# A decoder layer on one core: the mixer's x1 goes straight to the output tensor, and the last stage adds the expert sums to it with accumulating stores

## The chip, the core and the metric

The kernel runs on one core of a Trainium2 chip. The core has five engines that run side by side and wait for each other by semaphores: PE (TensorE, matrix multiply), DVE (VectorE, elementwise), ACT (ScalarE, activation functions), POOL (GpSimd) and SP (SyncE, which here only issues transfers). Sixteen DMA engines, shared by all who issue transfers, move data between the core's own memory (SBUF, 128 partitions) and the chip's main memory (DRAM). The metric is the time of one execution on the device, in microseconds (us).

## What is computed

One layer of a decoder, 2048 tokens of 1024 f32 values each:

```python
h = rms_norm(x, g_pre_mix) * (1.0 + sc1) + sh1
proj = h @ w_in
y = concat([conv_module(...), hgrn2(...)]) @ w_out
x = x + gt1 * rms_norm(y, g_post_mix)            # this x is "x1" below

h = rms_norm(x, g_pre_ffn) * (1.0 + sc2) + sh2
y = hier_moe(h, ...)                             # per token 2 of 32 experts, weighted sum
x = x + gt2 * rms_norm(y, g_post_ffn)            # the output
```

`rms_norm(y, g)` is `y * rsqrt(mean(y*y) + 1e-6) * g`, one mean per token. The last line is what the changed stage computes: `x1 + grow2 * y / rms(y)`, with `grow2 = gt2 * g_post_ffn`, a row of 1024 values.

## The kernel before

The work is cut into 16 tiles of 128 tokens; a tile of 128 x 1024 f32 is 0.524 MB (512 KB), 4 KB in each partition. Four phases follow one another, each in a block of its own that all engines leave together.

**Mixer** (`mixer_phase`, to about 1210 us). Four blocks of 512 tokens. Here x1 is made on DVE in the tile `yt`, and POOL stores it to DRAM (L321, 16 stores), stores the normalised `xn` (L323) and clears the tensor `y` in DRAM with zeros (L325). `ap["x1"]` names the DRAM tensor that takes x1: an internal tensor `x1_dram`.

**Routing** (`routing_phase`, to about 1265 us) chooses two experts for each token and lists blocks of 128 rows by expert.

**Experts** (`expert_phase`, about 1265 to 1789 us). 48 blocks run. For each, POOL fetches 128 rows of `xn` with an indirect transfer (L1547). PE turns them and multiplies by the expert's gate and up weights (L1614 to L1616), then by the down weights (L1626). The product, weighted on ACT, is added to `y` in DRAM by an indirect transfer that accumulates, issued by POOL (L1563). That is an `indirect_dma_start` with `compute_op=ALU.add`. Each of these waits for the one before it. The weights of an expert are 3 MB (gate 1 MB, up 1 MB, down 1 MB), loaded by SP into three slots (L1428, L1429, L1434) once an earlier expert has left its slot. In SP's program, after every three experts, comes one `load_x1` (L1504). It brings two tiles of x1, 1 MB, from DRAM into `x1_all`, an SBUF array that holds all 16 tiles. There are 8 of these loads.

**Combine** (`combine_phase`, from about 1789 us). SP loads `y` tile by tile into a ring of 8 places `ys` (L1850). Per tile, ACT squares and sums it (L1829), takes a logarithm (L1831) and an exponential (L1833), which gives the reciprocal of the root of the mean. DVE multiplies the tile by that and by `grow2` (L1842), then adds it to the x1 tile in SBUF (L1845). SP stores the result to `out` (L1856) and then issues the load of the tile 8 places on.

SP's and ACT's transfers run on the queue that the trace calls q1, POOL's on q0. Both are served by the same 16 DMA engines.

Of the kernel before, what the change touches and what calls it, by code (L numbers as in the profile page):

```python
# [4 lines left out]
F32 = mybir.dt.float32  # L5
# [4 lines left out]
ALU = mybir.AluOpType  # L10
ACT = mybir.ActivationFunctionType
AX = mybir.AxisListType

P = 128
D = 1024
KD = D // P
SEQ = 2048
# [9 lines left out]
NTILES = SEQ // P  # L27
# [28 lines left out]
def wait_apart(eng, sem, value, passed):  # L56

    eng.wait_ge(sem, value)
    eng.sem_inc(passed, 1)
# [1128 lines left out]
def routing_phase(nc, ap, c):  # L1188

    with ExitStack() as ctx:  # L1190
# [19 lines left out]
        rowf, blkf = sb("rowf", [P, NA]), sb("blkf", [P, NA])  # L1210
        RING = 8
        at_row, at_blk = sb("at_row", [P, RING, P]), sb("at_blk", [P, RING, TAB])
        dest = sb("dest", [P, 2, NTILES], I32)
# [27 lines left out]
        def _(pool):  # L1241
# [16 lines left out]
            for n in range(3, NA, 4):  # L1258
                if n >= RING:
                    pool.wait_ge(onehot_used, (n - RING) // 4 + 1)  # L1260
                nc.gpsimd.tensor_scalar(at_blk[:, n % RING], blk[:], blkf[:, n:n + 1], assign[:, n:n + 1],
                                        ALU.is_equal, ALU.mult).then_inc(fourth_ready, 1)
# [15 lines left out]
        def _(pe):  # L1278
# [9 lines left out]
            for n in range(NA):  # L1288
                if n % 4 == 0:
                    pe.wait_ge(onehot_ready, n // 4 * 3 + 3)  # L1290
                    pe.wait_ge(fourth_ready, n // 4 + 1)
                last = nc.tensor.matmul(pi[:, 0:TAB], at_row[:, n % RING], at_blk[:, n % RING], start=(n == 0), stop=(n == NA - 1))
                if n % 4 == 3:
# [131 lines left out]
def load_gate_up(eng, ap, c, e, s):  # L1425

    w = lambda name: ap[name][0][bass.ds(e, 1)].rearrange("a (k p) n -> p (a k) n", p=P)
    eng.dma_start(c.wgu[:, s, :, 0:FE], w("w_gate")).then_inc(c.gu_in[s], 16)  # L1428
    eng.dma_start(c.wgu[:, s, :, FE:2 * FE], w("w_up")).then_inc(c.gu_in[s], 16)  # L1429
# [7 lines left out]
def expert_phase(nc, ap, c):  # L1437

    with ExitStack() as ctx:
        sb = lambda n, s, d=F32: ctx.enter_context(nc.sbuf_tensor(n, s, d))  # L1440
        sem = lambda n: ctx.enter_context(nc.semaphore(n))
# [28 lines left out]
        pool_passed, sp_passed = c.pool_passed, c.sp_passed  # L1470
        block = ctx.enter_context(nc.Block())
# [9 lines left out]
        @block.sync  # L1481
        def _(sp):
            expert_at = lambda r: sp.value_load(c.rank_expert[0:1, bass.ds(r, 1)], min_val=0, max_val=NE - 1)
            end_of = lambda r: sp.value_load(c.rank_end[0:1, bass.ds(r, 1)], min_val=0, max_val=NBLK)

            def announce(loaded, landed, n):
                sp.wait_ge(landed, n)
                sp.sem_inc(loaded, 1)

            def next_gate_up(r, s):  # L1490

                e = expert_at(r + WSLOTS)
                wait_apart(sp, w_rest_ready, 4 * end_of(r) + 1, sp_passed)
                load_gate_up(sp, ap, c, e, s)

            def next_down(r, s):

                e = expert_at(r + WSLOTS)
                wait_apart(sp, y_ready, 2 * end_of(r) + 1, sp_passed)
                load_down(sp, ap, c, e, s)  # L1500

            def load_x1(n):

                sp.dma_start(c.x1_all[:, bass.ds(2 * n, 2)], ap["x1"][bass.ds(2 * n * P, 2 * P), :]  # L1504
                             .rearrange("(t p) n -> p t n", p=P)).then_inc(c.x1_in, 16)

            def gate_up_landed(r, s, turn):
                announce(gate_up_loaded, c.gu_in[s], 32 * turn)

            def down_landed(r, s, turn):  # L1510
                announce(down_loaded, c.wd_in[s], 16 * turn)

            def serve(r, s, turn):
                known = isinstance(r, int)
                after, turn_after = (s + 1) % WSLOTS, turn + (s + 1) // WSLOTS
                if not known or r + 1 < NE:
                    gate_up_landed(r + 1, after, turn_after)
                if not known or r + WSLOTS < NE:
                    next_gate_up(r, s)
                if known and r == WSLOTS - 1:  # L1520
                    for n in range(WSLOTS - 1):
                        next_down(n, n)
                elif not known or WSLOTS <= r < NE - WSLOTS + 1:
                    next_down(r - 1, (s - 1) % WSLOTS)
                if not known or r + 1 < NE:
                    down_landed(r + 1, after, turn_after)

            ROUNDS = NTILES // 2
            gate_up_landed(0, 0, 1)
            down_landed(0, 0, 1)  # L1530
            for s in range(WSLOTS):
                serve(s, s, 1)
            load_x1(0)
            with sp.Fori(1, ROUNDS) as g:
                for s in range(WSLOTS):
                    serve(g * WSLOTS + s, s, g + 1)
                load_x1(g)
            for r in range(ROUNDS * WSLOTS, NE):
                serve(r, r % WSLOTS, r // WSLOTS + 1)

# [266 lines left out]
def combine_phase(nc, ap, c, out):  # L1807

    with ExitStack() as ctx:
        sb = lambda n, s, d=F32: ctx.enter_context(nc.sbuf_tensor(n, s, d))  # L1810
        sem = c.sem
        RING = 8
        ys = sb("ys", [P, RING, D])
        junk = sb("junk", [P, D])
        ss = sb("ss", [P, RING])
        y_in = [sem(f"y_in{s}") for s in range(RING)]
        out_stored, squared, logged, rstd_ready, gated, out_ready = (
            sem(n) for n in ("out_stored", "squared2", "logged", "rstd_ready", "gated", "out_ready"))
        sp_passed = c.sp_passed
        block = ctx.enter_context(nc.Block())  # L1820

        @block.scalar
        def _(act):
            A = nc.scalar.activation
            act.preload_act_table_set("natural_log_exp_and_others")
            for i in range(NTILES):
                s = i % RING
                act.wait_ge(y_in[s], 16 * (i // RING + 1))
                A(junk[:], ys[:, s], ACT.Square, accum_out=ss[:, s:s + 1]).then_inc(squared, 1)  # L1829
                act.wait_ge(squared, i + 1)  # L1830
                A(ss[:, s:s + 1], ss[:, s:s + 1], ACT.Ln, bias=c.epsc[:], scale=1.0 / D).then_inc(logged, 1)  # L1831
                act.wait_ge(logged, i + 1)
                A(ss[:, s:s + 1], ss[:, s:s + 1], ACT.Exp, scale=-0.5).then_inc(rstd_ready, 1)  # L1833

        @block.vector
        def _(dve):
            V = nc.vector
            dve.wait_ge(c.x1_in, NTILES // 2 * 16)
            for i in range(NTILES):
                s = i % RING  # L1840
                dve.wait_ge(rstd_ready, i + 1)  # L1841
                V.scalar_tensor_tensor(out=ys[:, s], in0=ys[:, s], scalar=ss[:, s:s + 1], in1=c.grow2[:],  # L1842
                                       op0=ALU.mult, op1=ALU.mult).then_inc(gated, 1)
                dve.wait_ge(gated, i + 1)
                V.tensor_tensor(c.x1_all[:, i], c.x1_all[:, i], ys[:, s], ALU.add).then_inc(out_ready, 1)  # L1845

        @block.sync
        def _(sp):
            def load(i):
                sp.dma_start(ys[:, i % RING], ap["y"][i * P:(i + 1) * P, :]).then_inc(y_in[i % RING], 16)  # L1850

            for i in range(RING):
                load(i)
            for i in range(NTILES):
                wait_apart(sp, out_ready, i + 1, sp_passed)
                sp.dma_start(out[i * P:(i + 1) * P, :], c.x1_all[:, i]).then_inc(out_stored, 16)  # L1856
                if i + RING < NTILES:
                    load(i + RING)
            sp.wait_ge(out_stored, NTILES * 16)


INPUTS = ["x", "c", "w_ada", "b_ada", "g_pre_mix", "g_post_mix", "w_in", "dw_kernel", "dw_bias",
# [8 lines left out]
def build(nc, ap, out):  # L1871
    c = Kept()
    c.mixer_sems = []
    with ExitStack() as ctx:
        sb = lambda n, s, d=F32: ctx.enter_context(nc.sbuf_tensor(n, s, d))
# [4 lines left out]
        c.gcol = sb("gcol", [P, 2 * KD])  # L1880
        c.logits = sb("logits", [P, NTILES, NR])
        c.pool_passed, c.sp_passed = (ctx.enter_context(nc.semaphore(n)) for n in ("pool_passed", "sp_passed"))
        ap["x1"] = nc.dram_tensor("x1_dram", (SEQ, D), F32, kind=DEBUG_KIND).ap()
        ap["xn"] = nc.dram_tensor("xn_dram", (SEQ, D), F32, kind=DEBUG_KIND).ap()
        ap["y"] = nc.dram_tensor("y_dram", (SEQ + P, D), F32, kind="Internal").ap()
        ap["weight"] = nc.dram_tensor("weight_dram", (2 * SEQ, 1), F32, kind="Internal").ap()
        with ExitStack() as mix:
# [8 lines left out]
            c.state = mb("state", [P, 4, DC])  # L1896
            c.scoreT = mb("scoreT", [P, 2, DC])
            mixer_phase(nc, ap, c)
        c.x1_all, c.grow2 = sb("x1_all", [P, NTILES, D]), sb("grow2", [P, D])
        c.sem = lambda n: ctx.enter_context(nc.semaphore(n))  # L1900
        c.x1_in = c.sem("x1_in")
        with ExitStack() as moe:
            eb = lambda n, s, d=F32: moe.enter_context(nc.sbuf_tensor(n, s, d))
            c.block_token, c.block_assign = eb("block_token", [P, TAB], I32), eb("block_assign", [P, TAB], I32)
# [9 lines left out]
            routing_phase(nc, ap, c)  # L1914
            expert_phase(nc, ap, c)
        combine_phase(nc, ap, c, out[0])


DEBUG_KIND = "Internal"
# [17 lines left out]
```

## Time and profile before

| | |
|---|---|
| time, median of 3 runs | 1842.37 us (1840.76 to 1842.48) |
| time of the profiled execution | 1839.05 us |
| its span, first to last instruction | 1837.5 us |
| mean granted TensorE clock | 0.914 of full |
| PE busy | 1533.9 us, 83% of the span |
| DVE busy | 1296.4 us, 71% |
| ACT busy | 841.1 us, 46% |
| POOL busy | 374.0 us, 20% |
| DMA, queue q1 (SP, ACT) | 193.03 MB, 31.4% of 16 engines |
| DMA, queue q0 (POOL) | 97.19 MB, 18.9% of 16 engines |

The profile records one execution. A busy time is the sum over an engine's instructions. For a DMA queue it is the time that its packets took, as a share of what 16 engines have in the stretch. Where a share is near 100% the DMA engines had no time left. An average over the span mixes phases with different limits, so the stretch that a change touches has to be read by itself.

### The profile page before, as it was taken

What the parts mean: (1) busy time and instruction counts of PE and PEld (TensorE: products, weight loads), DVE (VectorE), ACT (ScalarE), POOL (GpSimd) and SP (SyncE); (2) the same over time, 40 slices, a digit from 0 to 9 for tenths busy, and PEclk for the clock granted to TensorE, in tenths of its full rate; (3) what the DMA queues carried; (4) which work ended last, traced back from release to release, by engine and by line L of the source; (5) the groups of instructions that cost most, each with busy time, mean ns of one, the idle gap of its engine ahead of it and who ended that gap; (6) DMA issues with size and microseconds to landing.
All of it is one profiled execution on the core that took longest, in us unless ns stands there. A gap on an engine that the chain in (4) does not pass through costs nothing. (4 is left out here: it accounts for less than half of the span.)

```text
span 1837.5 us, 24383 instructions
## 1 busy us (share of the span) xinstructions
PE 1533.9 (83%) x7268; PEld 1152.0 (63%) x7270; DVE 1296.4 (71%) x1999; ACT 841.1 (46%) x1443; POOL 374.0 (20%) x403
## 2 busy tenths in 40 slices
PE   2597945699998899998899998926989999999960
PEld 2486824488855789666689475425667666666730
DVE  5489966679965499865599652257667877778738
ACT  1422232433363522454322542313767787878745
POOL 1000000000010000010000010114546666665640
PEclk9999966799998899998899998956989999999985
DMA  9255114133322232322331122372999998889948
GB/s 341 76 157 187 52 43 163 64 94 107 98 81 71 81 110 73 92 92 92 84 100 47 38 89 81 126 237 82 314 338 301 302 341 263 241 229 315 279 97 363
DMA packets 200424, 291.29 MB, mean 159 GB/s; under 512 B 10558, under 2 KB 158171, under 8 KB 200346
## 3 DMA queue, kind: packets, MB, share of 16 engines
q1 hardware_dynamic: 169762, 193.03, 31.4%
q0 software_dynamic: 30416, 97.19, 18.9%
q8 instruction: 45, 0.74, 0.2%
q14 instruction: 33, 0.27, 0.0%
q10 hardware_dynamic: 168, 0.06, 0.0%
HBM read 240.42 MB, written 59.26 MB: 163 GB/s over the span
## 5 line engine op out<-in xcount | busy, mean ns | idle before, releaser
L892 DVE SCALAR_TENSOR_TENSOR cv<-u,taps,cv 128x512 f32<-128x512 f32 x480 | 321.7, 743 | 0.6 <-DVE yT L848 0.3
L1741 DVE TENSOR_TENSOR w_rest<-wgu,w_high 128x1024 fp32r<-128x1024 f32 x192 | 233.7, 1221 | 94.5 <-ACT w_high L1666 93.3
L1666 ACT ACTIVATE w_high<-wgu 128x1024 fp32r x192 | 201.5, 1054 | 139.3 <-PE pgu L1616 86.0
L416 PE MATMUL bank<-hT_high,tiles_operand 128*128 128x512 f32 x512 | 204.6, 400 | 35.7 <-DVE hT_operand L866 21.1
L417 PE MATMUL bank<-hT_operand,tiles_operand 128*128 128x512 f32 x512 | 203.2, 397 | 0.0
L418 PE MATMUL bank<-hT_high,win_operand 128*128 128x512 f32 x512 | 202.9, 396 | 0.0
L439 PE MATMUL bank<-wo,yT 128*128 128x512 f32 x432 | 189.7, 594 | 0.0
L1626 PE MATMUL py<-wd,hTe 128*128 x384 | 172.6, 592 | 0.9 <-ACT yb L1693 0.9
L1614 PE MATMUL pgu<-w_high,x_high 128*128 128x512 f32 x384 | 155.3, 404 | 0.0
L1616 PE MATMUL pgu<-w_high,x_rest 128*128 128x512 f32 x384 | 151.0, 393 | 0.0
L1615 PE MATMUL pgu<-w_rest,x_high 128*128 128x512 f32 x384 | 151.0, 393 | 0.0
L425 PE MATMUL bank<-tiles_operand,hT_high 128*128 128x256 f32 x512 | 145.7, 285 | 4.4 <-DVE win_operand L871 4.4
L427 PE MATMUL bank<-tiles_operand,hT_operand 128*128 128x256 f32 x512 | 145.6, 284 | 0.0
L426 PE MATMUL bank<-win_operand,hT_high 128*128 128x256 f32 x512 | 145.6, 284 | 0.0
L439 PEld LDWEIGHTS bank<-wo,yT 128*128 128x128 f32 x432 | 81.2, 191 | 96.8 <-issue 96.8
L416 PEld LDWEIGHTS bank<-hT_high,tiles_operand 128*128 128x128 f32 x512 | 98.7, 193 | 58.4 <-issue 31.9
L305 POOL DMA_DIRECT2D tiles<-x_in x16 | 8.7, 543 | 553.6 <-PE bank L427 491.0
L871 DVE TENSOR_TENSOR win_operand<-win,tiles_operand 128x2048 fp32r<-128x2048 f32 x48 | 109.7, 2286 | 15.5 <-ACT tiles_operand L630 15.5
L1626 PEld LDWEIGHTS py<-wd,hTe 128*128 128x128 f32 x384 | 72.5, 189 | 73.8 <-issue 70.1
L1563 POOL DMA_INDIRECT y_dram<-yb,places x48 | 89.5, 1865 | 120.4 <-DMA y_dram<-yb,places 77.5
L417 PEld LDWEIGHTS bank<-hT_operand,tiles_operand 128*128 128x128 f32 x512 | 98.8, 193 | 20.7
L418 PEld LDWEIGHTS bank<-hT_high,win_operand 128*128 128x128 f32 x512 | 98.5, 192 | 21.1
(345 smaller groups left out, 2910.4 us busy)
## 6 DMA issues: line engine op xcount, KB each, us to landing
win<-w_in_in SPq DMA_DIRECT2D x64, 512.0 KB, 5.2
wgu<-w_gate_in SPq DMA_DIRECT2D x32, 1024.0 KB
wgu<-w_up_in SPq DMA_DIRECT2D x32, 1024.0 KB
wd<-w_down_in SPq DMA_DIRECT2D x32, 1024.0 KB
wo<-w_ada_in POOLq DMA_DIRECT2D x8, 2048.0 KB, 9.2
win<-w_in_in SPq DMA_DIRECT2D x16, 1024.0 KB, 5.2
y_dram<-zeros POOLq DMA_DIRECT2D x17, 512.0 KB, 5.3
win<-x_in SPq DMA_DIRECT2D x16, 512.0 KB, 4.5
```

The source lines that it names most:

```text
L416: nc.tensor.matmul(out[:], high[:, k, cols], hT_high[:, k, :], start=(k == 0), stop=False)
L417: nc.tensor.matmul(out[:], high[:, k, cols], hT_rest[:, k, :], start=False, stop=False)
L418: last = nc.tensor.matmul(out[:], rest[:, k, cols], hT_high[:, k, :], start=False, stop=(k == KD - 1))
L425: nc.tensor.matmul(to, hT_high[:, k, tok], high[:, k, :], start=(k == 0), stop=False)
L439: last = nc.tensor.matmul(out[:], yT[:, k, i * P:(i + 1) * P], wo[:, k, half * 512:(half + 1) * 512], start=(k == 0), stop=(k == KD - 1))
L892: ins = V.scalar_tensor_tensor(out=cv[:, j], in0=u[:, j, w:w + T], scalar=tap, in1=cv[:, j], op0=ALU.mult, op1=ALU.add)
L1614: nc.tensor.matmul(pgu[s][:], x_high[:, k, :], w_high[:, k, :], start=(k == 0), stop=False)
L1615: nc.tensor.matmul(pgu[s][:], x_high[:, k, :], w_rest[:, k, :], start=False, stop=False)
L1616: last = nc.tensor.matmul(pgu[s][:], x_rest[:, k, :], w_high[:, k, :], start=False, stop=(k == KD - 1))
L1626: last = nc.tensor.matmul(py[half][:], hT[:, k, :], c.wd[:, bass.ds(slot, 1), k, half * 512:(half + 1) * 512].rearrange("p a n -> p (a n)" ...
L1666: A(w_high[:, QK * q:QK * q + QK, :], c.wgu[:, bass.ds(slot, 1), QK * q:QK * q + QK, :].rearrange("p a k n -> p (a k) n"), ACT.Copy).then_ ...
L1741: V.tensor_tensor(w_rest[:, part, :], c.wgu[:, bass.ds(slot, 1), part, :].rearrange("p a k n -> p (a k) n"), w_high[:, part, :].bitcast(F3 ...
```

## The change

The mixer's x1 now goes into the kernel's output tensor: `ap["x1"]` is `out[0]`. The internal tensor, the SBUF array `x1_all`, its semaphore and the 8 loads in the expert phase are gone. In the combine phase `ys` holds all 16 tiles, and SP issues the 16 loads at once. DVE multiplies each tile and no longer adds. POOL stores each tile to `out` with `accum_op=ALU.add`, so that the transfer itself adds the tile to the x1 that lies there.

```diff
@@ -1499,11 +1499,6 @@
                 wait_apart(sp, y_ready, 2 * end_of(r) + 1, sp_passed)
                 load_down(sp, ap, c, e, s)
 
-            def load_x1(n):
-
-                sp.dma_start(c.x1_all[:, bass.ds(2 * n, 2)], ap["x1"][bass.ds(2 * n * P, 2 * P), :]
-                             .rearrange("(t p) n -> p t n", p=P)).then_inc(c.x1_in, 16)
-
             def gate_up_landed(r, s, turn):
                 announce(gate_up_loaded, c.gu_in[s], 32 * turn)
 
@@ -1530,11 +1525,9 @@
             down_landed(0, 0, 1)
             for s in range(WSLOTS):
                 serve(s, s, 1)
-            load_x1(0)
             with sp.Fori(1, ROUNDS) as g:
                 for s in range(WSLOTS):
                     serve(g * WSLOTS + s, s, g + 1)
-                load_x1(g)
             for r in range(ROUNDS * WSLOTS, NE):
                 serve(r, r % WSLOTS, r // WSLOTS + 1)
 
@@ -1809,14 +1802,12 @@
     with ExitStack() as ctx:
         sb = lambda n, s, d=F32: ctx.enter_context(nc.sbuf_tensor(n, s, d))
         sem = c.sem
-        RING = 8
-        ys = sb("ys", [P, RING, D])
+        ys = sb("ys", [P, NTILES, D])
         junk = sb("junk", [P, D])
-        ss = sb("ss", [P, RING])
-        y_in = [sem(f"y_in{s}") for s in range(RING)]
-        out_stored, squared, logged, rstd_ready, gated, out_ready = (
-            sem(n) for n in ("out_stored", "squared2", "logged", "rstd_ready", "gated", "out_ready"))
-        sp_passed = c.sp_passed
+        ss = sb("ss", [P, NTILES])
+        y_in = [sem(f"y_in{i}") for i in range(NTILES)]
+        out_stored, squared, logged, rstd_ready, gated = (
+            sem(n) for n in ("out_stored", "squared2", "logged", "rstd_ready", "gated"))
         block = ctx.enter_context(nc.Block())
 
         @block.scalar
@@ -1824,39 +1815,32 @@
             A = nc.scalar.activation
             act.preload_act_table_set("natural_log_exp_and_others")
             for i in range(NTILES):
-                s = i % RING
-                act.wait_ge(y_in[s], 16 * (i // RING + 1))
-                A(junk[:], ys[:, s], ACT.Square, accum_out=ss[:, s:s + 1]).then_inc(squared, 1)
+                act.wait_ge(y_in[i], 16)
+                A(junk[:], ys[:, i], ACT.Square, accum_out=ss[:, i:i + 1]).then_inc(squared, 1)
                 act.wait_ge(squared, i + 1)
-                A(ss[:, s:s + 1], ss[:, s:s + 1], ACT.Ln, bias=c.epsc[:], scale=1.0 / D).then_inc(logged, 1)
+                A(ss[:, i:i + 1], ss[:, i:i + 1], ACT.Ln, bias=c.epsc[:], scale=1.0 / D).then_inc(logged, 1)
                 act.wait_ge(logged, i + 1)
-                A(ss[:, s:s + 1], ss[:, s:s + 1], ACT.Exp, scale=-0.5).then_inc(rstd_ready, 1)
+                A(ss[:, i:i + 1], ss[:, i:i + 1], ACT.Exp, scale=-0.5).then_inc(rstd_ready, 1)
 
         @block.vector
         def _(dve):
             V = nc.vector
-            dve.wait_ge(c.x1_in, NTILES // 2 * 16)
             for i in range(NTILES):
-                s = i % RING
                 dve.wait_ge(rstd_ready, i + 1)
-                V.scalar_tensor_tensor(out=ys[:, s], in0=ys[:, s], scalar=ss[:, s:s + 1], in1=c.grow2[:],
+                V.scalar_tensor_tensor(out=ys[:, i], in0=ys[:, i], scalar=ss[:, i:i + 1], in1=c.grow2[:],
                                        op0=ALU.mult, op1=ALU.mult).then_inc(gated, 1)
-                dve.wait_ge(gated, i + 1)
-                V.tensor_tensor(c.x1_all[:, i], c.x1_all[:, i], ys[:, s], ALU.add).then_inc(out_ready, 1)
 
         @block.sync
         def _(sp):
-            def load(i):
-                sp.dma_start(ys[:, i % RING], ap["y"][i * P:(i + 1) * P, :]).then_inc(y_in[i % RING], 16)
-
-            for i in range(RING):
-                load(i)
             for i in range(NTILES):
-                wait_apart(sp, out_ready, i + 1, sp_passed)
-                sp.dma_start(out[i * P:(i + 1) * P, :], c.x1_all[:, i]).then_inc(out_stored, 16)
-                if i + RING < NTILES:
-                    load(i + RING)
-            sp.wait_ge(out_stored, NTILES * 16)
+                sp.dma_start(ys[:, i], ap["y"][i * P:(i + 1) * P, :]).then_inc(y_in[i], 16)
+
+        @block.gpsimd
+        def _(pool):
+            for i in range(NTILES):
+                wait_apart(pool, gated, i + 1, c.pool_passed)
+                pool.dma_start(out[i * P:(i + 1) * P, :], ys[:, i], accum_op=ALU.add).then_inc(out_stored, 16)
+            pool.wait_ge(out_stored, NTILES * 16)
 
 
 INPUTS = ["x", "c", "w_ada", "b_ada", "g_pre_mix", "g_post_mix", "w_in", "dw_kernel", "dw_bias",
@@ -1880,7 +1864,7 @@
         c.gcol = sb("gcol", [P, 2 * KD])
         c.logits = sb("logits", [P, NTILES, NR])
         c.pool_passed, c.sp_passed = (ctx.enter_context(nc.semaphore(n)) for n in ("pool_passed", "sp_passed"))
-        ap["x1"] = nc.dram_tensor("x1_dram", (SEQ, D), F32, kind=DEBUG_KIND).ap()
+        ap["x1"] = out[0]
         ap["xn"] = nc.dram_tensor("xn_dram", (SEQ, D), F32, kind=DEBUG_KIND).ap()
         ap["y"] = nc.dram_tensor("y_dram", (SEQ + P, D), F32, kind="Internal").ap()
         ap["weight"] = nc.dram_tensor("weight_dram", (2 * SEQ, 1), F32, kind="Internal").ap()
@@ -1896,9 +1880,8 @@
             c.state = mb("state", [P, 4, DC])
             c.scoreT = mb("scoreT", [P, 2, DC])
             mixer_phase(nc, ap, c)
-        c.x1_all, c.grow2 = sb("x1_all", [P, NTILES, D]), sb("grow2", [P, D])
+        c.grow2 = sb("grow2", [P, D])
         c.sem = lambda n: ctx.enter_context(nc.semaphore(n))
-        c.x1_in = c.sem("x1_in")
         with ExitStack() as moe:
             eb = lambda n, s, d=F32: moe.enter_context(nc.sbuf_tensor(n, s, d))
             c.block_token, c.block_assign = eb("block_token", [P, TAB], I32), eb("block_assign", [P, TAB], I32)
```

In SP's program for the expert phase, the loop body over three experts ends as follows (`wd` are the down weights; a minus marks a row of before, a plus one of the changed kernel):

```order
 L1434 DMA wd<-w_down_in 128x2x1024
 L1487 REGISTER_ALU
-L1504 ISA
-L1504 REGISTER_ALU
-L1504 DMA x_all<-x_dram 128x2x1024
-L1534 REGISTER_ALU
-L1534 COMPARE_AND_BRANCH
+L1528 REGISTER_ALU
+L1528 COMPARE_AND_BRANCH
```

The x1 load is gone from the loop, and nothing takes its place there; the loads of weights keep their order.

At the end of SP's program, in the combine phase, the last rows of before and all of after are these:

```order
-L1850 DMA ys<-y_dram 128x1024
-L1856 DMA out<-x_all 128x1024
-L1850 DMA ys<-y_dram 128x1024
-L1856 DMA out<-x_all 128x1024 x8
-L1809 UNCONDITIONAL_BRANCH
+L1833 UNCONDITIONAL_BRANCH
+L1836 DMA ys<-y_dram 128x1024 x16
+L1802 UNCONDITIONAL_BRANCH
```

Loads and stores alternated from the ninth load on; now the 16 loads stand in one row and no store is on SP.

The end of POOL's program (the first two rows close the expert phase in both kernels):

```order
 L58 REGISTER_ALU
 L1439 UNCONDITIONAL_BRANCH
+L1838 UNCONDITIONAL_BRANCH
+L1842 DMA out<-ys 128x1024 x16
+L1802 UNCONDITIONAL_BRANCH
```

POOL had nothing to do in the combine phase and now issues the 16 accumulating stores.

## Rows read from the trace of the kernel before

**Rows 1.** Busy time by stretch (start:end, length, engines, PEclk, DMA share, GB/s):

```profile
core 0: us, PE busy (x) PEld busy (x) DVE busy (x) ACT busy (x) POOL busy (x), PEclk, DMA share, GB/s
1400.00:1600.00 200.00, 198.42 (x828) 139.09 (x827) 158.67 (x238) 160.74 (x260) 127.65 (x118) 1.00 0.95 287
...
1780.00:1800.00 20.00, 0.00 (x0) 0.00 (x0) 4.87 (x5) 7.14 (x15) 0.69 (x1) 0.50 0.59 187
1800.00:1838.00 38.00, 0.00 (x0) 0.00 (x0) 33.93 (x29) 19.85 (x51) 0.00 (x0) 0.50 0.88 358
```

**Rows 2.** The chain that ended last, 1740 to 1838 us (start, us, what):

```profile
by line: DVE x_all L1845 20.0%; DVE ys L1842 19.8%; DMA ys<-y_dram 3.3%; ACT junk L1829 1.2%; issue 0.6%; ACT ss L1831 0.3%; ACT ss L1833 0.2%; DVEq L1841 0.0%
...
1789.95 3.27 DMA ys<-y_dram
...
1833.19 1.22 DVE x_all L1845
```

**Rows 3.** Groups of instructions, 1788 to 1838 us (xcount | busy us, mean ns | idle before):

```profile
L1842 DVE SCALAR_TENSOR_TENSOR ys<-ys,ss,grow 128x1024 f32<-128x1024 f32 x16 | 20.4, 1277 | 24.2 <-ACT ss L1833 24.2
L1845 DVE TENSOR_TENSOR x_all<-x_all,ys 128x1024 f32<-128x1024 f32 x16 | 19.6, 1225 | 0.6
L1829 ACT ACTIVATE junk<-ys 128x1024 f32<-128x1024 f32 x16 | 16.8, 1052 | 8.2 <-DMA ys<-y_dram 8.2
L1831 ACT ACTIVATE ss<-ss,epsc 128x1 f32<-128x1 f32 x16 | 4.7, 294 | 0.5
L1833 ACT ACTIVATE ss<-ss 128x1 f32<-128x1 f32 x16 | 3.2, 203 | 0.5
L1829 ACT ACTIVATION_READ_ACCUMULATOR junk<-ys 128x1 f32 x16 | 3.0, 187 | 0.0
```

**Rows 4.** DMA queues, 1816 to 1826 us (packets, MB, share of 16 engines):

```profile
DMA packets 1155, 4.21 MB, mean 421 GB/s; under 512 B 128, under 2 KB 128, under 8 KB 1155
...
q1 hardware_dynamic: 1155, 4.21, 102.8%
```

**Rows 5.** DMA queues, 1788 to 1792 us:

```profile
q1 hardware_dynamic: 67, 0.27, 21.1%
```

**Rows 6.** DMA queues, 1311 to 1313 us:

```profile
q0 software_dynamic: 99, 0.40, 100.5%
q1 hardware_dynamic: 23, 0.06, 7.6%
```

**Rows 7.** DMA queues, 1773 to 1779 us (GB/s in 40 slices of 0.15 us):

```profile
GB/s 0 0 0 0 0 0 0 273 164 0 82 137 109 27 55 109 137 191 109 191 218 191 191 246 164 273 137 273 82 82 55 0 0 0 0 0 0 0 0 0
...
q0 software_dynamic: 144, 0.52, 58.8%
```

**Rows 8.** DMA queues, 1270 to 1790 us:

```profile
q1 hardware_dynamic: 70384, 99.62, 55.2%
q0 software_dynamic: 15446, 41.72, 35.3%
```

**Rows 9.** POOL's issues: timeline (start, us), and one line's durations (ns min/median/max):

```profile
1779.10 1.59 POOL L1563 DMA_INDIRECT y_dram<-yb,places  x1 [5.34 <-DMA y_dram<-yb,places]
...
L325 POOL DMA_DIRECT2D y_dram<-zeros x16: 1133/1158/1170, 527.0 to 1205.8; - x16
```

**Rows 10.** PE's timeline, line L1633, once per block (start, us, [idle before <-releaser]):

```profile
1336.47 0.38 PE L1633 MATMUL ph<-ident,hh 128*128 128x128 f32 x2
1350.31 0.69 PE L1633 MATMUL ph<-ident,hh 128*128 128x128 f32 x2 [3.67 <-DVE hh L1760]
1365.19 0.44 PE L1633 MATMUL ph<-ident,hh 128*128 128x128 f32 x2 [1.98 <-DVE hh L1760]
1376.86 0.38 PE L1633 MATMUL ph<-ident,hh 128*128 128x128 f32 x2
...
1446.86 0.38 PE L1633 MATMUL ph<-ident,hh 128*128 128x128 f32 x2
1456.86 0.38 PE L1633 MATMUL ph<-ident,hh 128*128 128x128 f32 x2
```

**Rows 11.** DMA busy tenths, 1310 to 1375 us; then line L1504, all 8:

```profile
DMA  9999999999999999999999999999999999999999
...
L1504 SPq DMA_DIRECT2D x_all<-x_dram x8: 387/395/2062, 1309.9 to 1655.5; - x8
```

## The prediction

> **What bounds the kernel now.** I read first the busy time by stretch. In the expert phase, 1400 to 1600 us, PE is busy 198.4 of 200 us and the DMA engines 0.95 of the time [rows 1]: two resources are nearly full at once, and a transfer more or less there may or may not count. After 1780 us PE does nothing; DVE is busy 33.9 of 38 us and DMA 0.88 at 358 GB/s [rows 1]. The combine phase therefore stands at the end, beside nothing, and all of it counts.
>
> Second, the chain that ended last. From 1789.95 us it goes through the first load of `y` (3.27 us) and one tile on ACT, and from there DVE's two lines take it to the end: L1842 and L1845 hold 19.8% and 20.0% of the stretch, and the last add ends at 1834.4 us [rows 2]. DVE's 16 products take 20.4 us and its 16 additions 19.6 us, with 0.6 us of gaps [rows 3].
>
> Third, what lies just under DVE. DMA queue q1 moves 4.21 MB in 10 us with its packets covering 102.8% [rows 4]. That is the plain price: 0.524 MB per tile at 0.421 MB/us is 1.25 us of all 16 engines. Sixteen loads and sixteen stores cost 32 x 1.25 = 40.0 us, just as much as DVE's 40.0. ACT already waits 8.2 us for loads [rows 3]. Freeing DVE alone can gain only the few us by which the two ends differ; what decides is what the new stores cost the DMA engines.
>
> **The removed work.** DVE loses 19.6 us of additions. Its remaining chain is short: ACT needs 1.052 + 0.187 + 0.294 + 0.203 = 1.74 us per tile, so 16 tiles from 1793.2 end by 1821, and DVE's product of the last (1.28) by 1822.3 [rows 2, 3]. SP's stores leave its queue, and it waits for nobody in the phase. These edits by themselves set no end, because DMA covers them up to the end worked out below.
>
> **The accumulating store.** The combine phase has none, but the expert phase has 48 accumulating transfers of the same size, 128 rows of 4 KB (L1563). They are indirect, the new ones are not; what each row costs the DMA engine is the nearest that there is. Three readings:
> - Backlog: from 1311 to 1313 us q0 has 99 packets of accumulate, 0.40 MB, at 100.5% of the engines, with almost nothing of q1 (7.6%) [rows 6]. At 0.20 MB/us a tile costs 2.6 us, twice the plain 1.25.
> - Alone: one between 1773 and 1779 us takes 58.8% of 6 us, 3.5 us, and its rate climbs from 82 to over 200 GB/s in the course of it [rows 7]: the start of a transfer is slow.
> - Mean over the phase: q0 is 35.3% of 520 us, 183.6 us, for 41.72 MB [rows 8]. 48 accumulates are 25.2 MB; the other 16.5 MB are gathers, at the plain 0.42 MB/us 39.4 us. (183.6 - 39.4) / 48 = 3.0 us.
>
> In the new phase stores queue behind one another, which is the backlog case; I take 2.7 us, near the first reading, and keep 2.6 and 3.5 as bounds. 16 x 2.7 = 43.2 us.
>
> The Trainium skill, "DMA: Bandwidth & Descriptors", in Anatomy of one DMA, prices a transfer issued by GpSimd at about 2.0 us fixed plus bytes / 436e9, whatever it does with the bytes; by that rule the fixed part overlaps between queued stores and a store would cost 1.2 us of the engines like a plain one. Its Rules for kernel authors say that an accumulate reads its destination and writes it later, which is one more trip than that formula counts. The trace sides with the second: 0.20 MB/us against 0.42 [rows 4, 6].
>
> **Issue.** POOL's plain issues take 1.16 us, its indirect accumulate 1.59 [rows 9]. Sixteen are 19 to 26 us, hidden under the 43 us of data; POOL has no other work there and no one waits for it. Without that cover they would end near 1796.3 + 26 = 1822 us, with the products.
>
> **The sum of the combine phase.** By 1792 us the loads had moved 0.27 MB [rows 5], so they count as running at full rate from 1792 - 0.27/0.42 = 1791.4. All 16 loads are issued at once, and the first store joins at 1793.2 + 1.74 + 1.28 + 1.59 (issue) = 1797.8, so the engines are never idle from there: 1791.4 + 20.0 (loads) + 43.2 (stores). In the lone accumulate data stops at 1777.65 (slice 31 of 40), and the next, which waits for it, is issued at 1779.10 [rows 7, 9]; about 1.45 us is the landing, so the end is 1856.05 against the span's 1837.5: **+18.5 us**. With 2.6 it is +17, with 3.5 it is +31.4.
>
> **The expert phase.** The 8 loads of x1 are 8.4 MB, 2 x 1.25 = 2.5 us of DMA each, issued between 1309.9 and 1655.5 [rows 11]. A block takes PE 10.00 us when nothing is late (1446.86 to 1456.86), but 13.84, 14.88 and 11.67 us from 1336 to 1377 [rows 10], 10.4 us lost, and over all of 1310 to 1375 the DMA engines are full [rows 11]: there the weights are late. The loads of x1 that go into that stretch, the first (1309.9) and the second (one loop of three experts later), put 5.0 us ahead of weights. Taking them out should return them: **-5 us**. The other six fall where PE mostly runs at its 10.00; they are worth nothing while PE covers them. Bounds: 0, if the slots and not the bytes set when weights arrive; 8, with small delays later on.
>
> **Mixer.** The 16 stores of x1 go to another DRAM tensor, in the same places of POOL's queue, with the same sizes: nothing.
>
> **Total.** +18.5 - 5 = +13.5 us. The sum is made against the profiled execution (span 1837.5, time 1839.05, so 1.55 us around it); the median of the runs lies 3.3 us above that execution, and I add the difference to the median: 1842.37 + 13.5 = 1856 us. In the profile the span would be about 1851.
>
> **Rivals.**
> - *Stores at the plain price (faster), 9 in 100.* If queued accumulates overlap their read of the destination with other packets, 32 x 1.25 us is all: 1791.4 + 40.0 + 1.45 = 1832.9, 4.65 us under the span of before; with the experts' -5 the time is 1842.37 - 9.65 = 1832.7 us. DVE's 19.6 us would be gone without price, and the engines' floor would end the phase. The point from which it decides is a store of 1.84 us: 16 x 1.84 + 20 + 1791.4 + 1.45 - 5 = 1837.3. The stretch with full engines speaks against it, since there 2.6 us was paid with other packets waiting in the queue [rows 6]. This is also where the skill's formula would lead, with the number just given; so far the trace gives it little.
> - *Stores dearer than in the backlog (slower still), 14 in 100.* If every store pays as the lone one, 3.5 us, the phase ends at 1868.9, +31.4, and without gain among the experts the time is 1874 us; with it 1869. For it: two queues alternating, and reads and writes of the same DRAM rows. Against it: rows 6.
> - *No gain among the experts, within the forecast's case, 1 in 4 of it.* The combine phase alone: 1842.37 + 18.5 = 1861 us.
> - *A draw, 5 in 100.* A store between 1.6 and 2.1 us leaves the time within 3.7 us of before.
>
> **How the numbers follow.** My forecast's case (stores 2.6 to 3.1 us, experts 0 to -8) has 72 in 100, the rest being the dear stores 14, the plain price 9 and the draw 5. With 2.6 and -8 it gives 1842.4 + 17 - 8 = 1851, with 3.1 and 0 1842.4 + 24.9 = 1867. The range reaches above to the lone price, 1874, and below to 1846, where a store costs about 2.3 us. A measurement tells about 0.2%, 3.7 us, from no change. Slower 0.86, within it 0.05, faster 0.09.
>
> **What would show it.** In the changed profile: DVE in the combine phase busy about 20 us and off the chain, the DMA engines full from 1791 to the end at some 265 GB/s on average (16.8 MB in 63 us), the chain ending in DMA to `out`, q0 near 0.20 MB/us once the loads have landed. In the expert phase the blocks between 1340 and 1377 shorter, by 5 us in all, and the last block ending that much earlier. The prediction falls if q0 then moves 0.4 MB/us, or if POOL's issues stand apart by more than 2.7 us with idle DMA engines between them.

## The result and the profile after

| | before | changed |
|---|---|---|
| median of 5 runs | 1841.59 us (1839.91 to 1842.48) | 1850.76 us (1849.65 to 1851.54) |
| ratio to before | | 1.005, 95% interval 1.0035 to 1.0064 |
| profiled execution, span | 1837.5 us | 1849.8 us |

The change makes the kernel slower by 0.5%, 9.2 us. It lies inside the range of 1846 to 1874 and 5 us under the forecast of 1856.

The stretches of the changed kernel's combine phase, with the columns of [rows 1]: the whole, from SP's first load, then three parts of it.

```profile
1784.50:1849.80 65.30, 0.00 (x0) 0.00 (x0) 20.55 (x16) 26.98 (x65) 13.87 (x16) 0.50 0.99 257
1784.50:1795.00 10.50, 0.00 (x0) 0.00 (x0) 4.44 (x4) 8.18 (x18) 2.16 (x3) 0.50 0.91 339
1795.00:1829.00 34.00, 0.00 (x0) 0.00 (x0) 14.27 (x12) 17.16 (x44) 9.99 (x12) 0.50 1.05 276
1829.00:1849.80 20.80, 0.00 (x0) 0.00 (x0) 1.84 (x2) 1.65 (x4) 1.72 (x2) 0.50 0.93 185
```

DVE is busy 20.55 of 65.3 us and the DMA engines 0.99. The counted rate falls from 339 GB/s, nearly loads alone, to 276 where both queues run, to 185 at the end. The work of DVE went, and the phase grew from 47.5 us (1789.95 to 1837.5) to 65.3 (1784.54 to 1849.8).

The chain that ended last, by share of the stretch from 1740 us, and the piece of it where the time is:

```profile
by line: DMA ys<-y_dram 34.4%; SPq L1836 6.6%; issue 1.2%; DVE ys L1830 1.2%; ACT junk L1819 1.1%; POOL out L1842 0.8%; ACT ss L1821 0.3%; ACT ss L1823 0.2%; POOLq L59 0.0%
...
1792.43 37.88 DMA ys<-y_dram
```

In [rows 2] it was DVE's two lines. Now it is a load of `y`: the last one is issued at 1792.43 and lands 37.9 us later. In that time the accumulating stores run beside the loads and the counted rate is 276 GB/s. The groups of the phase, with the columns of [rows 3]:

```profile
L1830 DVE SCALAR_TENSOR_TENSOR ys<-ys,ss,grow 128x1024 f32<-128x1024 f32 x16 | 20.5, 1284 | 47.3 <-ACT ss L1823 47.3
L1819 ACT ACTIVATE junk<-ys 128x1024 f32<-128x1024 f32 x16 | 16.8, 1051 | 19.5 <-DMA ys<-y_dram 19.5
L1842 POOL DMA_DIRECT2D out<-ys x16 | 13.9, 867 | 45.7 <-DVE ys L1830 45.7
```

DVE waits for ACT, ACT for loads, POOL for DVE. POOL's issues take 0.87 us each and 13.9 in all, so they bound nothing.

What a store costs is read where no load is in flight, 1835 to 1840 us, and over the phase (DMA queues: packets, MB, share of 16 engines):

```profile
q0 software_dynamic: 289, 1.05, 106.3%
```

```profile
q0 software_dynamic: 2304, 8.39, 64.6%
q1 hardware_dynamic: 2304, 8.39, 34.4%
```

The first line is from 1835 to 1840 us, the other two from 1784.5 to 1849.8. 1.05 MB in 5 us is 0.21 MB/us, 2.5 us per tile, against 1.25 for a plain one [rows 4]. Over the phase the stores took 64.6% and the loads 34.4% of 65.3 us for the same bytes.

In the expert phase, PE's line once per block, to be read against [rows 10]:

```profile
1337.41 0.38 PE L1626 MATMUL ph<-ident,hh 128*128 128x128 f32 x2
1347.48 0.44 PE L1626 MATMUL ph<-ident,hh 128*128 128x128 f32 x2
1359.38 0.44 PE L1626 MATMUL ph<-ident,hh 128*128 128x128 f32 x2 [1.29 <-DVE hh L1753]
1369.48 0.38 PE L1626 MATMUL ph<-ident,hh 128*128 128x128 f32 x2
```

The steps are 10.07, 11.90 and 10.10 us where they were 13.84, 14.88 and 11.67. SP's first load of `y` comes at 1784.54, 5.4 us earlier.

### The profile page after: what moved, and what is told of

It reads as the page before. It is cut to its first block and busy times, and to the rows that moved or that the text cites. A ratio compares the mean times of both kernels' runs of the same rounds, so it can differ in the third digit from the quotient of the medians.

```text
span 1849.8 us, 24337 instructions
## 1 busy us (share of the span) xinstructions
PE 1532.1 (83%) x7268; PEld 1150.3 (62%) x7270; DVE 1278.6 (69%) x1983; ACT 841.5 (45%) x1443; POOL 390.6 (21%) x419
```

## The experiments

Each run is compared with the kernel before in the same runs. "Phase" is the combine phase of the profiled execution, from SP's first load of `y` to the end of the span; "expert stretch" is the time from the first to the last of PE's 48 lines for a block, 488.4 us in the profile of before and 481.6 in that of the changed kernel.

| version | median us | ratio, 95% interval | phase us | expert stretch us |
|---|---|---|---|---|
| changed | 1850.76 | 1.0050 (1.0035 to 1.0064) | 65.3 | 481.6 |
| stores without the addition | 1831.67 | 0.9944 (0.9928 to 0.9961) | 46.0 | 482.1 |
| changed, x1 loads kept | 1858.86 | 1.0099 (1.0080 to 1.0118) | 66.0 | 486.5 |
| x1 loaded in the combine phase | 1848.96 | 1.0042 (1.0028 to 1.0057) | 65.2 | 482.5 |
| x1 loaded early | 1831.20 | 0.9946 (0.9931 to 0.9962) | 47.4 | 482.8 |
| each store twice | 1892.48 | 1.0272 (1.0252 to 1.0292) | 107.6 | 482.6 |
| early, POOL adds 5 tiles | 1836.92 | 0.9968 (0.9957 to 0.9978) | 51.5 | 481.1 |
| early, again | 1832.34 | 0.9944 (0.9929 to 0.9958) | 47.5 | 481.1 |
| before, again (one run) | 1841.24 | | 47.5 | 490.4 |
| first two loads kept | 1839.40 | 0.9994 (0.9985 to 1.0003) | 47.6 | 486.6 |
| last six loads kept | 1831.04 | 0.9951 (0.9937 to 0.9964) | 47.6 | 480.4 |
| two small loads in their place | 1832.69 | 0.9962 (0.9948 to 0.9976) | 47.7 | 482.1 |
| first two loads halved | 1835.64 | 0.9982 (0.9971 to 0.9993) | 47.6 | 483.1 |

**Stores without the addition.** It tells the addition from the queue that carries it. The output lacks x1.

```diff
-                pool.dma_start(out[i * P:(i + 1) * P, :], ys[:, i], accum_op=ALU.add).then_inc(out_stored, 16)
+                pool.dma_start(out[i * P:(i + 1) * P, :], ys[:, i]).then_inc(out_stored, 16)
```

> The changed kernel, but POOL's 16 stores in the combine phase overwrite the output instead of adding to it, so x1 is missing from the output. Theory A (the addition itself doubles what a store costs the DMA engines, 2.5 us instead of 1.25): the phase from the first load's issue to the end falls from 65.3 us to about 43 (20 us of loads, 20 us of stores, 3 us of start and landing), and the time from 1851 to about 1829 us. Theory B (POOL's queue, or the two queues taking turns, makes the stores slow): the phase stays near 65 us and the time near 1851.

Measured: 1831.67 us and a phase of 46.0. Its DMA queues from 1784 to 1830 us:

```profile
q1 hardware_dynamic: 2304, 8.39, 48.3%
q0 software_dynamic: 2304, 8.39, 44.6%
```

The same packets and bytes on the same queue now cost 44.6% of 46 us, 20.5, where they cost 64.6% of 65.3, 42.2. The addition is the price; POOL's queue and the turns are not. The phase is 3 us longer than expected: the last data moves at about 1827.8 and the span ends at 1830.0, so a store on POOL's queue needs 2.2 us to land and be waited for. Before, with stores on SP's queue, data stopped at about 1836.6 and the span ended at 1837.5, 0.9 us later. Counted to the last data, the phase fell from 46.7 to 43.8 us, by 2.9; counted to the end of the span by 1.5.

**Changed, with the loads of x1 kept.** The expert phase's part of the change undone alone (SP waits for these loads, long landed, before it loads `y`).

```diff
+            load_x1(0)
             with sp.Fori(1, ROUNDS) as g:
                 for s in range(WSLOTS):
                     serve(g * WSLOTS + s, s, g + 1)
+                load_x1(g)
```

> The changed kernel with the 8 loads of x1 back in the expert phase, at their old places, into an array that nobody reads afterwards. Theory A (these loads delay weights between 1310 and 1377 us): the time grows by about 5 us, to 1856, with the blocks of that stretch at 13 to 15 us again. Rival (the earlier end of the expert phase in the changed kernel's profile came from chance in how the weights arrived, not from the loads): no growth, 1851 within 2.

Measured: 1858.86 us, ratio 1.0099 against the changed kernel's 1.0050, so the loads cost about 9 us in the timed runs. In the profile the expert stretch is 486.5 us, 4.9 more than the changed kernel's. The explanation by chance falls, and the cost is larger than the 5 us expected.

**x1 loaded in the combine phase.** The kernel before without the loads of the expert phase; no accumulating store, the second read is an ordinary load. The first edit stands in the function that loads a tile of `y`.

```diff
+                if i % 2:
+                    sp.dma_start(c.x1_all[:, i - 1:i + 1], ap["x1"][(i - 1) * P:(i + 1) * P, :]
+                                 .rearrange("(t p) n -> p t n", p=P)).then_inc(x1_pair[i // 2], 16)
...
+                dve.wait_ge(x1_pair[i // 2], 16)
```

> The kernel before, but x1 comes into SBUF in the combine phase, in 8 loads of 1 MB beside those of y, and not in the expert phase. DVE adds, SP stores plainly. Theory A (an accumulating store costs just what a plain store and a plain load of the same rows cost): DMA needs 16 x (1.25 + 1.25 + 1.25) = 60 us as in the changed kernel, so the time is that of the changed kernel, 1851 within 3. If the addition in the DMA engines costs something beyond its second read, this one is faster than the changed kernel; if the second read is cheaper than a load, it is slower.

Measured: 1848.96 us, phase 65.2 against 65.3, expert stretch 482.5. The DMA queues from 1784 to 1849.2 us:

```profile
q1 hardware_dynamic: 6784, 25.17, 96.7%
```

25.17 MB, three times 8.39, in 65.2 us. The changed kernel moved the same, only that its queue counts 16.78 of them. An accumulating store costs what a store and a load cost.

**x1 loaded early.** The saving of the expert phase without its price.

```diff
             for e in range(WSLOTS):
                 load_gate_up(sp, ap, c, e, e)
                 load_down(sp, ap, c, e, e)
+            for n in range(NTILES // 2):
+                sp.dma_start(c.x1_all[:, 2 * n:2 * n + 2], ap["x1"][2 * n * P:(2 * n + 2) * P, :]
+                             .rearrange("(t p) n -> p t n", p=P)).then_inc(c.x1_in, 16)
```

> The kernel before, but all 8 loads of x1 stand in the routing phase, behind the first weights, where the trace of before shows idle DMA engines from about 1242 to 1263 us; 8.4 MB take 20 us there. Theory A: the expert phase gains its 5 us as in the changed kernel and the combine phase keeps its 47.5 us, so the time is 1841.6 - 5 = 1837 us. Rival (the 5 us are chance, or the early loads delay the first rows and weights of the experts): 1841 or more.

Measured: 1831.20 us, ratio 0.9946, and later 1832.34, 0.9944. This beats before by 10 us and the changed kernel by 19. PE's line in the repeat:

```profile
1339.73 0.38 PE L1634 MATMUL ph<-ident,hh 128*128 128x128 f32 x2
1349.73 0.38 PE L1634 MATMUL ph<-ident,hh 128*128 128x128 f32 x2
1359.73 0.38 PE L1634 MATMUL ph<-ident,hh 128*128 128x128 f32 x2
```

Blocks stand 10.00 us apart in the stretch that held the late ones [rows 10]. In the first profile of this version one step there still took 11.52 us. The gain in time is twice the expected 5 us.

**Each store twice.** The suspected cost doubled.

```diff
                 pool.dma_start(out[i * P:(i + 1) * P, :], ys[:, i], accum_op=ALU.add).then_inc(out_stored, 16)
+                pool.dma_start(ap["xn"][i * P:(i + 1) * P, :], ys[:, i], accum_op=ALU.add).then_inc(out_stored, 16)
```

> The changed kernel, with each of the 16 accumulating stores followed by a second accumulating store of the same tile to xn in DRAM, which nobody reads any more. Theory A (a queued accumulating store costs the DMA engines 2.5 us each, and they are what the combine phase waits for): 16 x 2.5 = 40 us more, the phase 65 + 40 = 105 us, the time about 1851 + 40 = 1891. Rival (part of the phase is POOL's issuing, or the waiting of ACT for late loads, which a second store would hide under): clearly under 40 us more, 25 or less.

Measured: 1892.48 us, 41.7 above the changed kernel's 1850.76 (expected 40), phase 107.6 against 65.3. Its DMA from 1860 to 1880 us:

```profile
DMA packets 1156, 4.21 MB, mean 211 GB/s; under 512 B 128, under 2 KB 128, under 8 KB 1156
```

4.21 MB in 20 us, where [rows 4] has 4.21 MB in 10. Nothing of the second store hid under anything.

**POOL adds five tiles.** What freeing DVE is worth with plain stores.

```diff
+                if i % 3 != 1:
                     dve.wait_ge(gated, i + 1)
                     V.tensor_tensor(c.x1_all[:, i], c.x1_all[:, i], ys[:, s], ALU.add).then_inc(out_ready, 1)
...
+        @block.gpsimd
+        def _(pool):
...
+            for i in range(1, NTILES, 3):
+                pool.wait_ge(gated, i + 1)
+                nc.gpsimd.tensor_tensor(c.x1_all[:, i], c.x1_all[:, i], ys[:, i % RING], ALU.add).then_inc(pool_ready, 1)
```

> The version with early loads of x1, and of the 16 additions in the combine phase POOL makes 5 (every third tile), DVE 11. It asks what freeing DVE is worth by itself, with plain stores. Theory A (DMA needs 40 us there as DVE does, so DVE's time is worth only what it ends after DMA): the phase gets 1 to 2 us shorter than the 47.4 of the version with early loads alone, which the timing can hardly tell. Rival (DVE was the bound and the DMA engines had room): DVE's 6.1 us less show fully, a phase of about 41 us and a time 6 us lower.

> The version with the loads of x1 in the routing phase once more, beside the one in which POOL adds some tiles. Its expert phase is to be compared with that of before again. The profiles so far have the expert phase 5 to 6 us shorter without the loads of x1, the timed runs 9 to 10 us. If the timed runs are right, this one is again about 10 us below before, 0.9945 of it; if the profile is, about 5 us, 0.997.

The repeat of the early loads gave 1832.34 us, 0.9944 of before, as the timed runs had it. For the first version both cases of the expectation missed: 1836.92 us, 4.6 slower than the early loads alone beside it, and a phase of 51.5 against 47.5. The timeline of the phase from 1790 to 1804 us, DVE and then POOL:

```profile
1790.41 1.23 DVE L1848 TENSOR_TENSOR x_all<-x_all,ys 128x1024 f32<-128x1024 f32 x1
...
1794.17 3.26 DVE L1848 TENSOR_TENSOR x_all<-x_all,ys 128x1024 f32<-128x1024 f32 x1
```

```profile
1792.99 3.35 POOL L1855 TENSOR_TENSOR x_all<-x_all,ys 128x1024 f32<-128x1024 f32 x1 [18.25 <-DVE ys L1844]
```

DVE's addition took 3.26 us while POOL's ran, and 1.23 when it did not. Over the phase DVE's 11 additions took 23.6 us, more than its 16 had (19.6). The question of what a free DVE is worth was therefore not answered here. The version without the addition in the store gives 1.5 us, or 2.9 counted to the last data, as its stores land later on POOL's queue. No run has a free DVE with plain stores on SP's queue.

**Before, again.** No edit.

> The kernel before, unchanged, for a second profile of it. If the first profiled execution was a lucky one, the 47 steps from block to block on PE take more than its 488.4 us here, up to about 493; if it was an ordinary one, 488 within 1.

Measured: an expert stretch of 490.4 us, 2 above that of the first profile, between the two cases. The first profile was somewhat short, but one more profile cannot say how usual it was.

**Which of the eight loads.** Two kernels split them. The edit of the first, which brings the other six in the routing phase; the second leaves out `load_x1(0)` and the load in the first loop and has one in the second loop.

```diff
             load_x1(0)
-            with sp.Fori(1, ROUNDS) as g:
+            with sp.Fori(1, 2) as g:
                 for s in range(WSLOTS):
                     serve(g * WSLOTS + s, s, g + 1)
                 load_x1(g)
+            with sp.Fori(2, ROUNDS) as g:
+                for s in range(WSLOTS):
+                    serve(g * WSLOTS + s, s, g + 1)
```

> The kernel before with the first two loads of x1 at their old places in the expert phase and the other six in the routing phase. It asks which of the 8 loads cost the 6 us (profiles) or 10 us (timed runs) that all of them cost. Theory A, as the prediction had it (only the two that go into the stretch of 1310 to 1377 us with full DMA engines count): the time stays near that of before less 1 to 2 us, 1840, and the blocks of that stretch keep their 13 to 15 us. Rival (each load costs its share wherever it stands): about three quarters of the gain is there, 1834.

> The opposite: the first two loads of x1 in the routing phase, the other six at their old places in the expert phase. Theory A: nearly all of the gain, 1832 to 1834. Rival (each load costs its share): a quarter of it, 1839.

Measured: 1839.40 us with the first two kept (0.9994), 1831.04 with the last six kept (0.9951). The last six cost nothing that shows; the first two cost 8.4 us. PE's line with the first two kept:

```profile
1337.70 0.38 PE L1639 MATMUL ph<-ident,hh 128*128 128x128 f32 x2
1351.87 0.69 PE L1639 MATMUL ph<-ident,hh 128*128 128x128 f32 x2 [4.01 <-DVE hh L1766]
1365.72 0.44 PE L1639 MATMUL ph<-ident,hh 128*128 128x128 f32 x2 [0.92 <-DVE hh L1766]
1375.80 0.38 PE L1639 MATMUL ph<-ident,hh 128*128 128x128 f32 x2
```

The late blocks are back, 14.17 and 13.85 us; with the last six kept the steps from 1335.66 are 10.00, 10.42, 10.10 and 10.00.

The same stretch, with the columns of [rows 1], shows a second part of the loss. The lines are of before, of the first two kept and of the last six kept:

```profile
1336.00:1380.00 44.00, 38.35 (x147) 27.20 (x146) 27.53 (x42) 26.87 (x45) 18.31 (x21) 0.88 1.03 331
1336.00:1380.00 44.00, 39.07 (x155) 27.37 (x154) 28.74 (x46) 28.85 (x48) 20.30 (x23) 0.92 1.06 339
1336.00:1380.00 44.00, 43.75 (x189) 31.16 (x188) 33.98 (x51) 34.19 (x55) 27.71 (x27) 1.00 1.07 334
```

PE stands idle for 5.7 and 4.9 us of the 44 where the first two loads are kept, and for 0.3 where they are not. Its granted clock (PEclk) is 0.88 and 0.92 there against 1.00. Before, PE did nothing from 1346.6 to 1350.3 us, and from about 1349.0 to 1355.7 the granted clock was 0.50, the lower of its two levels (1.2 GHz). Two equal matmuls of before, one inside that time and one behind it:

```profile
1353.50 0.63 PE L1616 MATMUL pgu<-w_high,x_rest 128*128 128x512 f32 x1
1357.35 0.39 PE L1616 MATMUL pgu<-w_high,x_rest 128*128 128x512 f32 x1
```

The first took 0.63 us and the second 0.39. So a late load of weights costs twice: PE waits, and then works at the lower clock for some us.

**Bytes or place.** Small loads at the two places, and half of each.

```diff
+            def touch(n):
...
+                sp.dma_start(c.spare[:], ap["x1"][2 * n * P:(2 * n + 1) * P, 0:128]).then_inc(c.spare_in[n], 16)
```

```diff
-                sp.dma_start(c.x1_all[:, bass.ds(2 * n, 2)], ap["x1"][bass.ds(2 * n * P, 2 * P), :]
+                sp.dma_start(c.x1_all[:, bass.ds(2 * n, 1)], ap["x1"][bass.ds(2 * n * P, P), :]
```

> All of x1 comes in the routing phase; at the places of its first two loads in the expert phase SP issues a small load of 64 KB instead, into an array that nobody reads. The first two loads of x1 cost 8 to 10 us where they stood, though their bytes take the DMA engines 5.0 us. Theory C (bytes: what counts is the DMA time ahead of the weights): next to nothing of it is left, the time is within 2 us of the version with early loads, 1832, as this load has 1/16 of the bytes. Theory D (place: an issue there holds SP, which also announces landed weights and issues the next ones): the 8 to 10 us come back, 1840.

> As the version with the first two loads of x1 kept and six in the routing phase, but each of the two brings one tile (0.5 MB) and not two. Theory C (bytes): about half of the loss, 1835 to 1837. Theory D (place): the whole loss, 1840. A threshold (half fits into slack that the weights have) would show as no loss, 1832.

Measured: 1832.69 (0.9962) for the small ones and 1835.64 (0.9982) for the halves, between 0.9994 with both whole and 0.9944 to 0.9951 with none. The steps in the stretch are 10.00, 10.00, 10.10 with the small loads and 12.35, 11.92, 10.03 with the halves. The loss grows with the bytes. How evenly is less clear: beyond 10.00 us each, the steps lose 4.3 us with the halves and 8.1 with both whole, about half, while by the medians' ratios the halves keep 3.1 to 3.8 of 4.3 to 5.0 thousandths, with intervals of about 1 to either side. The small loads keep 1.1 to 1.8 thousandths, 2 to 3 us, with intervals that overlap those of none; a little may lie in the place.

## Why the prediction was right, point by point

- **DVE as the end, DMA just under it.** Right. With DVE's additions gone and the stores plain, the phase is 46.0 us instead of 47.5, or 43.8 instead of 46.7 counted to the last data. The 19.6 us that left DVE are worth 1.5 to 2.9.
- **DVE's products over by 1822.3.** Wrong, without effect on the sum. The last one ends at 1833.4, since ACT waited 19.5 us for loads that shared the DMA engines with stores. The DMA engines had work all the same, and the sum goes by them. The chain runs through a load of `y` and not, as the prediction had it, through the stores to `out`.
- **The accumulating store, 2.7 us, between 2.6 and 3.5.** Right in mechanism, the size 0.2 too high: 2.5 us. The reading from the backlog [rows 6] was the right one to choose, 0.20 MB/us against the measured 0.21; the mean over the expert phase (3.0) and the lone transfer (3.5) were not. For queued transfers one looks for a stretch in which the queue was full.
- **Two trips.** The Trainium skill, "DMA: Bandwidth & Descriptors", Rules for kernel authors, says that the accumulate reads its destination before it writes. The trace bears that out in amount: 65.3 us for 8.39 MB of loads and 8.39 of accumulating stores, 65.2 us for 25.17 MB of plain ones. Its Anatomy of one DMA counts bytes once, 0.524 MB / 436 GB/s or 1.2 us per store (an estimate by that page). The run with plain stores, near that price, had a phase of 46.0, and not 65.3.
- **The end of the phase.** Predicted 66.1 us from the first load's issue, measured 65.3. The stores were 16 x 0.2 = 3.2 us cheaper. Landing took about 2.4 instead of 1.45: data stops near 1847.4, the span ends at 1849.8. The rest, some 1.4 us, is not assigned.
- **Issue by POOL, hidden.** Right: 13.9 us under 42. The terms were too high, 1.16 and 1.59 us against 0.86. The 1.16 was read from the fill with zeros (L325); the stores of x1 (L321), the nearer kind, took 0.54 in the same trace.
- **The expert phase, -5 us.** The term of the sum that was mis-sized. The place was right: the first two loads carry the loss, the last six none that shows. The size was not: the 5.0 us of bytes were taken for the whole effect. In the timed runs it is 9 to 10 us: 1.0099 against 1.0050, and 0.9945 against 1. What the term left out, as the traces have it, is the clock. From 1336 to 1380 us PE is idle for 4.8 to 5.7 us in the four profiles with the first two loads in place, about the 5.0 of the bytes. The steps from block to block there lose more, 8.1 to 10.4 us, and the granted clock is 0.88 to 0.92. The missing share of the clock, 0.08 to 0.12 of 44 us, is 3.5 to 5.3 us by an estimate, and the steps lose 3.2 to 4.7 beyond the idle time. With the halves it is 2.4 us idle, a clock of 0.96 and 4.3 us lost; in the nine profiles with neither, 0 to 1.5 us idle, a clock of 1.00 and 0 to 2.1 lost. A term 4 to 5 us too small, a phase 0.8 us too long and a median of before that is now 0.8 lower (1841.59) cover the distance from 1856 to 1850.76.
- **The rivals.** Plain price: refuted by the run without the addition and by the doubled one. Dearer than in the backlog: refuted by 0.21 MB/us. No gain among the experts: refuted by the run that keeps the loads.

What stays open: the part of the clock is read from the traces, as no run held it up through the wait. And the whole expert stretch of the profiles shows 6 us (486.5 to 490.4 with the first two loads whole, 480.4 to 482.8 with none of them) where the steps after 1330 us show about 8 and the timed runs 9 to 10. One reason is in the steps before 1330 us, which lose 4.5 to 4.8 us in three of the four profiles with these loads and 6.9 to 8.5 in seven of the nine without. Another is which executions were profiled: before was profiled at 1839.05 and 1841.24 us and the early loads at 1834.97 and 1833.45, 5.9 us apart on average, where their medians are 9.6 and 10.5 apart. Whether either is chance is not shown.

## What to carry to other kernels

An addition that a store makes on its way is not free: it moves into the DMA engines as a second read, and pays only where they have room. A compute engine at the end of a chain is worth only the distance to the next resource under it, here 1.5 to 2.9 us of 19.6; so price that one before freeing the first. The useful half of this change was to take loads out of a stretch in which weights were late. That is had without the other half, by loading earlier: before, the DMA engines moved nothing from about 1243 to 1263 us. It gives 1831 to 1832 us, 0.9945 of before. And a wait on PE is to be priced with the clock that follows it: here 5 us of late bytes cost PE 8 to 10 us in the steps around them.

## What the hardware showed that was not expected

An addition of two SBUF tiles on DVE, 128x1024 f32, took 1.23 us alone and 3.26 us beside the same on POOL, which itself took 3.35. The Trainium skill, "SBUF — State Buffer", Who interferes with whom, says that a DVE instruction with two SBUF inputs contends with a GpSimd one that reads SBUF; the trace agrees. DVE's instruction ended 1.1 us after POOL's (1797.43 and 1796.34), nearly its own 1.23 us later, as if it had begun its work only then; this is read from these rows and was not tested. The 11 additions of DVE took 4.0 us more than its 16 alone, the phase grew by 4.0 us, and the expected gain became a loss of 4.6 us.

POOL's issue of a direct store took 0.53 us plain and 0.86 with the addition. From the last data to the end of the span passed about 2.2 to 2.4 us with stores on POOL's queue and 0.9 with stores on SP's.
